# Gates of the mLSTM through the split operands of the projection, the second group's h ahead of a weight split, and two V blocks through other PSUM banks

## The chip, the cores and the metric

One core of a Trainium2 chip runs the whole kernel. The metric is the device time of one execution in microseconds (us). Three executions of the kernel before gave 1976.03, 1974.39 and 1975.19 us; their median is 1975.19 us.

## The reference

One decoder layer (width 2048) for a prompt of 512 tokens and 8 samples of 8 tokens each, 576 tokens in all, in float32:

- `mod = silu(c) @ w_ada + b_ada`, cut into shift, scale and gate. There are 9 different conditions c, one for the prompt and one for each sample.
- `h = rmsnorm(x, norm_pre) * (1 + scale) + shift`, then `u = h @ w_in`. The columns of `u` are q, k, v, z of a differential attention, q, k, v, o, z of an mLSTM, two groups of 4 gate columns `i_m` and `f_m` (input and forget gate of the mLSTM's 4 heads), and two merge gates.
- The attention: 8 heads, two softmax maps each, ALiBi bias; causal within the prompt, and for the samples also over 256 cached keys taken from a paged cache.
- The mLSTM: `ig = i_m + b_igate`, `lf = log_sigmoid(f_m + b_fgate)`, then the recurrence over the tokens with a maximum stabiliser, starting from given states for the samples.
- Both branches are normed, gated and projected, merged by the sigmoids of the merge gates, projected by `w_out`, normed, gated and added to x.

Outputs are the new x, the new K and V rows and the final mLSTM states.

## The kernel before

**Split operands.** A float32 product is computed as three float32r matmuls: each operand is split into a high part (rounded to float32r) and a low part (the difference), and high by high, high by low and low by high are added in PSUM. `h_hi` and `h_lo` hold h as 16 tiles (`kt`) of 128 features by 576 tokens. Weights come in pieces of 256 rows by 256 columns into a ring of 4 slots: SyncE loads `w_raw`, ScalarE writes `w_hi` (`split_hi`), VectorE writes `w_lo` (`split_lo`, line 1514).

**Granules.** One piece is one granule on TensorE (lines 548 to 568): 2 column blocks (`cb`) by 2 row tiles (`t`) by 3 products by 2 halves of 288 tokens, 24 matmuls of 128x128 by 288. All matmuls are issued at line 546.

**The first phase (Q), groups of 4 granules.** h is not known at the start: `mod` is built chunk by chunk from `w_ada`, and chunk j gives shift and scale of the two feature tiles `2j` and `2j+1`. So the Q columns of `w_in` are walked in 8 groups (j = 0 to 7) of 4 granules (`q_granule(n)`, n = 4j + v), group j using tiles `2j` and `2j+1`. ScalarE (group 0) and VectorE (groups 1 to 7, `q_sum`) add each granule's result into `q_acc`. Beside them TensorE runs `ada_round`s, matmuls with 32 columns on one 128x32 strip of the array each (`bank_a`), which read `ada_in` as SyncE has loaded it. Rounds 4 to 7 lie behind granules 0 and 1; rounds 8 to 11 lie behind granule 4, and so on. A finished chunk is copied to `mod_rows` by VectorE (`ss_rows`), transposed by TensorE inside a granule (`ada_rows`, line 595) and folded into `mod_ss` by VectorE (`ss_out`, lines 1570 and 1573). Then `make_h(j)` (VectorE for j = 0 and 1, line 1608 on; GpSimd for j from 2) writes h of two tiles into `h_tmp`, ScalarE writes `h_hi` (`h_hi_pair`) and VectorE writes `h_lo` (`h_low`, line 1579).

**Gates.** `gates(j, ...)` (line 617) multiplies `h_tmp` in plain float32 by the 8 gate columns of `w_in`, padded to 32 (`w_pad`). Its 4 matmuls of 320 tokens go to the four strips of 32 partitions of `bank_s[:, 1]`: two feature tiles by two overlapping halves of the tokens. It stands ahead of the first granule of group j and waits for `h_made`; `make_h(j + 1)` waits for it, since it overwrites `h_tmp`. At granule 28 (`n == QN - 4`) VectorE copies the four strips to `g_rows`, and `gates_tokens` (line 627) adds and transposes them with a 0/1 matrix `g_pick`.

**Order of VectorE at group 0.** For each granule n: `early_lo(n + 3)` first, then in granule 2 `ss_out(1)` and `make_h(1)`, and in granule 3 `h_low(1)` ahead of `early_lo(6)`. ScalarE in granule 3: `h_hi_pair(1)`, then the two copies into `q_acc`, then `split_hi(6)`.

**V blocks and scores.** From x = 88 on (x counts granules of the later phase, 8 a pass p) attention steps are laid between granules: after each granule, transposes of step s-2 into `bank_a` (`weights_t`), the product with V of step s-3 into `bank_o` (`values`), and the scores of step s into both halves of `bank_s` (`scores`); A0 = 93 is step 0. After granules 96 and 97 (p = 12, g = 0 and 1) `to_tokens` also transposes a block of V from `stage` into `bank_s`; VectorE copies it out (`tok_v`, lines 1665 and 1666), and TensorE waits for that copy before the scores of the same step. ScalarE copies `bank_a` to `a_t` (`at_sb`) and `bank_o[:, 0:128]` to `att` (`pv_sb`).

Of the kernel before, what the change touches and what calls it, by code (L numbers as in the profile page):

```python
# [13 lines left out]
P = 128  # L14
# [101 lines left out]
def build(nc, x_prompt, x_sample, cache_k, cache_v, state_C, state_n, state_m, page_table, c_prompt, c_sample,  # L116
# [11 lines left out]
    with ctx:  # L128
# [106 lines left out]
        g_pick = sm("g_pick", [P, 2, 8])  # L235
# [26 lines left out]
        w_pad = sb("w_pad", "ROWS", 2 * KT * 9, [P, KT, 32])  # L262
# [7 lines left out]
        g_rows = sb("g_rows", "WORK", work[0], [P, GSPLIT + NS])  # L270
# [102 lines left out]
        pad_ready = sem("pad_ready")  # L373
        row_out = sem("row_out")
# [169 lines left out]
        def _(pe):  # L544
# [25 lines left out]
            def to_tokens(src, ready, free, dst=None):  # L570

                pe.wait_ge(*ready)
                pe.wait_ge(*free)
                for j in range(NT):
                    nc.tensor.transpose(bank_s[:, 0, j * P:(j + 1) * P], src[:, j * P:(j + 1) * P], ident[:])  # L575
                nc.tensor.transpose(bank_s[0:NS, 1, 0:P], src[:, TP:T], ident[:]).then_inc(dst, 1)
# [40 lines left out]
            def gates(j, jk, start, stop):  # L617

                pe.wait_ge(h_made, 2 * j + 2)
                for t in range(2):  # L620
                    for a in range(2):
                        q = 32 * (2 * t + a)
                        done = mm(bank_s[q:q + 32, 1, 0:GSPLIT + NS], w_pad[:, jk + t, :],
                                  h_tmp[:, t, a * GSPLIT:(a + 1) * GSPLIT + NS], start=start, stop=stop)
                done.then_inc(gates_mm, 1)

            def gates_tokens():

                pe.wait_ge(gate_vec, 1)
                for tt in range(NT + 1):  # L630
                    n, a = (P if tt < NT else NS), tt // 2 if tt < NT else 1
                    done = mm(bank_s[0:n, 0, tt * 8:(tt + 1) * 8], g_rows[:, tt * P - a * GSPLIT:tt * P - a * GSPLIT + n], g_pick[:, a, :])
                done.then_inc(gates_mm, 1)
# [21 lines left out]
            def q_granule(n):  # L655
                j, v = n // 4, n % 4
                if not v:
                    gates(j, 2 * j, j == 0, j == NG - 1)
                pe.wait_ge(h_lo_made, 2 * j + 1)
                pe.wait_ge(lo_ready, n + 1)  # L660
                more, rows_at = j < KG - 1, 1 if j else 2
                granule(n % RING, h_hi, h_lo, 2 * j, True, True, n if n else None, (h_lo_made, 2 * j + 2), j + 1 if v == rows_at and more else None)
                if j == 0 and v < 2:
                    for k in range(AQ + 2 * v, AQ + 2 * v + 2):
                        ada_round(k)
                if v == 0 and j and more:
                    for k in range(n + AQ, n + 2 * AQ):
                        ada_round(k)
# [20 lines left out]
            pe.wait_ge(in_wif, 16)  # L689
# [66 lines left out]
            for x in range(11 * NG, 16 * NG):  # L756
                p, g = x // NG, x % NG
                in_granule(p, g)
                if 0 <= x - A0 - 2 < STEPS:
                    weights_t(x - A0 - 2)  # L760
                if 0 <= x - A0 - 3 < STEPS:
                    values(x - A0 - 3)
                if p in (11, 12) and g < 2:
                    if p == 12:
                        pe.wait_ge(sc_max, x - A0)
                    to_tokens(stage[:, g, :], (bank_free[g], V0 + p), (tok_done, 2 * (p - 5) + g), tok_ps)
                    if p == 12:
                        pe.wait_ge(tok_done, 2 * (p - 5) + g + 1)
                if x == A0:
                    pe.wait_ge(k_kept, HA)  # L770
                if x == 11 * NG + 4:
                    pe.wait_ge(rows_exp, 1)
                    pe.wait_ge(tok_done, 14)
                    for i in range(NT + 1):
                        n = P if i < NT else NS
                        nc.tensor.transpose(bank_s[0:n, 1, 4 * i:4 * i + 4], row_g[:, i * P:i * P + n], ident[0:HM, 0:HM])
                        nc.tensor.transpose(bank_s[0:n, 1, 32 + 4 * i:36 + 4 * i], row_y[:, i * P:i * P + n], ident[0:HM, 0:HM])
                    nc.tensor.transpose(bank_s[0:NB, 1, 64:68], row_s[:, 3 * NS:3 * NS + NB], ident[0:HM, 0:HM]).then_inc(rows_tok_ps, 1)
                    pe.wait_ge(rows_tok, 1)
                if 0 <= x - A0 < STEPS:  # L780
                    scores(x - A0)
# [365 lines left out]
        def _(act):  # L1147
# [30 lines left out]
            act.wait_ge(pad_ready, 1)  # L1178
            act.dma_start(w_pad[:, :, 0:8], w_in2[:, COL_IF:COL_IF + 8].rearrange("(k p) c -> p k c", p=P)).then_inc(in_wif, 16)
# [29 lines left out]
            h_hi_pair(0)  # L1209
            for n in range(QN):  # L1210
# [295 lines left out]
        def _(dve):  # L1506
# [18 lines left out]
            V.memset(w_pad[:], 0.0)  # L1525
# [83 lines left out]
            def make_h(j):  # L1609
# [17 lines left out]
            h_low(0)  # L1627
            for n in range(1, LOOKAHEAD):
                early_lo(n)
            for n in range(QN):  # L1630
                c, v = n // 4, n % 4
                more = c < KG - 1
                if v == 3 and more:
                    h_low(c + 1)
                early_lo(n + LOOKAHEAD)
                if c:
                    q_sum(c, v, n, 0)
                if v == (1 if c else 2) and more:
                    ss_out(c + 1)
                    if not c:  # L1640
                        make_h(1)
# [21 lines left out]
            def tok_v(prompt, sample, n, blk):  # L1663
                dve.wait_ge(tok_ps, n + 1)
                V.tensor_copy(prompt[:, :, bass.ds(blk * P, P)], bank_s[:, 0, :].rearrange("p (a k) -> p a k", a=NT))
                V.tensor_copy(sample[:, bass.ds(blk * P, P)], bank_s[0:NS, 1, 0:P]).then_inc(tok_done, 1)
# [111 lines left out]
            for x in range(11 * NG, 16 * NG):  # L1778
                p, g = x // NG, x % NG
                if p in (11, 12) and g in (1, 2):  # L1780
                    tok_v(v_att, v_smp[0:NS, :], 2 * (p - 5) + g - 1, 2 * (p - 9) + g - 1)
                if x == 11 * NG + 5:
# [366 lines left out]
        def _(pool):  # L2149
# [15 lines left out]
            for a in range(2):  # L2165
                for t in range(2):
                    link(G.affine_select(out=g_pick[:, a, :], in_=g_pick[:, a, :], compare_op=ALU.not_equal, fill=1.0,
                                         base=-32 * (2 * t + a), pattern=[[-1, 8]], channel_multiplier=1))
# [40 lines left out]
            for j in range(2, NG):  # L2209
# [4 lines left out]
                pool.wait_ge(gates_mm, j)  # L2214
# [215 lines left out]
```

## Time and profile before

| | |
|---|---|
| median of 3 executions | 1975.19 us |
| profiled execution, own time | 1976.41 us |
| its span (first to last instruction) | 1974.9 us |
| TensorE busy | 1936.5 us (98%) |
| VectorE, ScalarE, GpSimd busy | 785.2, 642.2, 178.4 us (40%, 33%, 9%) |
| mean granted TensorE clock | 0.997 |

The span begins at the first instruction. "PE" is TensorE's matmuls, "PEld" its weight loads, which run beside the matmuls; the end of a matmul is modelled, so the distance between two starts is what one costs. A plain float32 matmul has two records. In a timeline a row is a run of like instructions, and the bracket gives how long the engine was idle before them and what ended that.

### The profile page before, as it was taken

How to read it: one execution, taken by the hardware profiler on the slowest of the kernel's cores; microseconds unless marked ns; L12 is line 12 of the kernel's file. 1: busy time of each engine (PE TensorE's matmuls, PEld its weight loads, DVE VectorE, ACT ScalarE, POOL GpSimd, SP SyncE). 2: the span in 40 equal slices, each digit the busy share in tenths (PEclk: the TensorE clock that was granted, in tenths of full speed). 3: DMA queues.
4: the chain of work that ended last, by engine and by line, in shares of the span. 5: the costliest groups of instructions: out<-in, count | busy, mean ns of one | idle time of the engine just before them, and what ended most of it. 6: DMA issues, size and time to landing. Idle time of an engine off the chain costs nothing.

```text
span 1974.9 us, 31160 instructions
## 1 busy us (share of the span) xinstructions
PE 1936.5 (98%) x12229; PEld 1661.8 (84%) x12229; DVE 785.2 (40%) x1679; ACT 642.2 (33%) x1144; POOL 178.4 (9%) x308
## 2 busy tenths in 40 slices
PE   6999999999999999999999999999999999999997
PEld 4789898988899998889899988878878878878885
DVE  4665234246553335454445322332332232353224
ACT  4222212235545454343243222222222222333332
POOL 2120012000020101122230000000000000010001
PEclk9999999999999999999999999999999999999998
DMA  9995662231234542223342332232232233353223
GB/s 310 314 290 185 206 225 79 79 107 54 54 121 142 173 138 73 78 82 110 96 131 80 82 84 80 82 103 85 80 104 80 84 102 85 121 189 98 80 81 122
DMA packets 166595, 240.52 MB, mean 122 GB/s; under 512 B 15145, under 2 KB 113577, under 8 KB 165305
## 3 DMA queue, kind: packets, MB, share of 16 engines
q1 hardware_dynamic: 150960, 194.03, 32.7%
q0 software_dynamic: 13264, 44.50, 6.9%
q8 instruction: 91, 1.49, 0.3%
q10 hardware_dynamic: 2242, 0.19, 0.1%
q14 instruction: 38, 0.31, 0.1%
HBM read 220.93 MB, written 17.73 MB: 121 GB/s over the span
## 4 chain that ended last, share of the span: by engine, by line
PE 75%; DVE 1%; POOL 1%; issue 1%; ACT 0%; DVEq 0%; ACTq 0%
PE gemm L546 59%; PE bank_s L546 9%; PE bank_o L546 2%; PE bank_a L546 2%; PE bank_s L795 1%; DVE g_m L2045 1%; DVE y_tok L2126 1%; PE bank_a L741 0%; PE bank_s L960 0%; POOL hm_sq L2343 0%; PE bank_s L1072 0%; POOL hm_sq L2342 0%; ACT hm_sq L1149 0%; PE bank_s L575 0%; DVE y_tok L2073 0%
## 5 line engine op out<-in xcount | busy, mean ns | idle before, releaser
L1514 DVE TENSOR_TENSOR w_lo<-w_raw,w_hi 128x512 fp32r<-128x512 f32 x512 | 358.4, 701 | 780.7 <-ACT w_hi L1149 780.2
L546 PE MATMUL gemm<-h_hi,w_hi 128*128 128x288 f32 (+1 forms) x2560 | 662.3, 324 | 3.5 <-DVE g_m L2045 1.7
L1149 ACT ACTIVATE w_hi<-w_raw 128x512 fp32r<-128x512 f32 x512 | 322.7, 631 | 1021.3 <-PE bank_s L546 568.7
L546 PE MATMUL gemm<-h_hi,w_lo 128*128 128x288 f32 (+1 forms) x2560 | 638.9, 315 | 0.0
L546 PE MATMUL gemm<-h_lo,w_hi 128*128 128x288 f32 (+1 forms) x2560 | 638.0, 314 | 0.0
L546 PEld LDWEIGHTS gemm<-h_hi,w_hi 128*128 128x128 f32 x2560 | 425.1, 189 | 81.4 <-issue 43.1
L546 PEld LDWEIGHTS gemm<-h_lo,w_hi 128*128 128x128 f32 x2560 | 425.5, 188 | 21.1
L546 PEld LDWEIGHTS gemm<-h_hi,w_lo 128*128 128x128 f32 x2560 | 425.8, 188 | 20.3
L546 PE MATMUL gemm<-w_hi,y_all 128*128 128x512 f32 x512 | 158.8, 391 | 0.6 <-DVE g_m L2045 0.6
L546 PEld LDWEIGHTS gemm<-w_hi,y_all 128*128 128x128 f32 x512 | 95.6, 188 | 24.9 <-DVE g_m L2045 1.4
L546 PE MATMUL gemm<-w_lo,y_all 128*128 128x512 f32 x256 | 99.9, 390 | 0.0
L546 PE MATMUL gemm<-brm,w_hi 128*128 128x512 f32 x256 | 79.4, 391 | 0.0
L546 PE MATMUL gemm<-bra,w_hi 128*128 128x512 f32 x256 | 79.4, 391 | 0.0
L2323 POOL DMA_DIRECT2D y_scratch<-g_a x12 | 6.5, 546 | 575.2 <-DVE g_a L2064 574.4
L546 PEld LDWEIGHTS gemm<-bra,w_hi 128*128 128x128 f32 x256 | 47.8, 188 | 11.8
L546 PEld LDWEIGHTS gemm<-brm,w_hi 128*128 128x128 f32 x256 | 47.7, 188 | 11.8 <-issue 0.2
L546 PEld LDWEIGHTS gemm<-w_lo,y_all 128*128 128x128 f32 x256 | 48.1, 188 | 10.2
L1801 DVE CUSTOM_DVE_ANT_0 e_map<-bank_s,alibi 128x128 f32<-128x128 f32 (+3 forms) x64 | 31.5, 492 | 55.3 <-PE bank_s L546 53.8
L546 PE MATMUL bank_s<-w_lo,h_smp 128*64 128x512 f32 x128 | 50.8, 397 | 0.0
L1149 ACT ACTIVATE e_map<-e_map,nmx 128x128 f32<-128x128 f32 (+3 forms) x64 | 35.6, 558 | 46.2 <-DVE nmx L1803 46.2
L546 PE MATMUL gemm<-brm,w_lo 128*128 128x512 f32 x128 | 50.0, 390 | 0.0
L546 PE MATMUL gemm<-bra,w_lo 128*128 128x512 f32 x128 | 50.0, 390 | 0.0
(458 smaller groups left out, 1749.7 us busy)
## 6 DMA issues: line engine op xcount, KB each, us to landing
w_raw<-in_w_in SPq DMA_DIRECT2D x384, 256.0 KB, 2.8
ada_in<-in_w_ada SPq DMA_DIRECT2D x72, 512.0 KB, 7.3
w_raw<-in_w_out SPq DMA_DIRECT2D x64, 256.0 KB, 2.4
ada_gate<-in_w_ada SPq DMA_DIRECT2D x16, 512.0 KB, 5.6
k_page<-in_cache_k POOLq DMA_DIRECT2D x16, 512.0 KB, 5.6
v_page<-in_cache_v POOLq DMA_DIRECT2D x16, 512.0 KB, 4.6
w_raw<-in_w_br_a SPq DMA_DIRECT2D x32, 256.0 KB, 2.4
w_raw<-in_w_br_m SPq DMA_DIRECT2D x32, 256.0 KB, 2.4
```

The lines of the kernel that those rows point to most:

```text
L546: return nc.tensor.matmul(out, lhsT, rhs, start=start, stop=stop, skip_group_check=True)
L795: done = nc.tensor.transpose(bank_s[:, j // 2, (j % 2 * PAGES + pg) * P:(j % 2 * PAGES + pg + 1) * P], k_page[:, pg, h * P:(h + 1) * P], i ...
L1149: return nc.scalar.activation(out, in_, func, **kw)
L1514: V.tensor_tensor(w_lo[:, slot], w_raw[:, slot], w_hi[:, slot], ALU.subtract).then_inc(lo_ready, 1)
L1801: link(V.tensor_tensor_reduce(e_map[:, s % 2, c, 0:n], bank_s[:, c, 0:n], alibi[:, TP - n:TP], 1.0, LOW, ALU.add, ALU.max, mx[:, s % 2, c: ...
L2045: ins = V.scalar_tensor_tensor(g, g, 1.0, gemm[:, b // 2, b % 2, :], ALU.add, ALU.mult)
L2126: V.scalar_tensor_tensor(y_tok[0:n, tt, half], y_tok[0:n, tt, half], rinv[0:n, tt:tt + 1], xa[0:n, half], ALU.mult, ALU.add).then_inc(fin_ ...
L2323: pool.dma_start(y_scratch[4 * i + b], g_a[:, b, :]).then_inc(y_stored, 16)
```

## The change

1. **Gates by split weights.** `w_pad` goes. The 8 gate columns are loaded into `w_if`; ScalarE writes their high part into columns 0 to 7 of `w_if_parts` and VectorE the low part into columns 8 to 15, each once. `gates(j)` now reads `h_hi` and `h_lo`: for two tiles and two halves, one float32r matmul with 16 columns on `h_hi` and one with 8 columns on `h_lo`, 8 in all, of 288 tokens, all to partitions 0 to 15 of the two halves of `bank_s`. It is issued behind the first granule of the group, ahead of the ada rounds. `make_h` no longer waits for it. The copy to `g_rows` is one of 16 partitions by 576, and `g_pick` has 16 rows.
2. **Second group's h.** In granule 2, VectorE does `ss_out(1)` and `make_h(1)` ahead of `early_lo(5)`.
3. **Two V blocks.** At p = 12 the transposes go to `bank_a` (prompt) and `bank_o[:, 128:256]` (samples). They wait for `at_sb` and `pv_sb`; the scores wait for nothing new, and the following `weights_t` waits for VectorE's copy.

```diff
+        w_if = sb("w_if", "ROWS", 2 * KT * 9, [P, KT, 8])
+        w_if_parts = sb("w_if_parts", "ROWS", 2 * KT * 9 + KT * 8, [P, KT, 16], F32R)
@@ TensorE
-            def to_tokens(src, ready, free, dst=None):
+            def to_tokens(src, ready, free, dst=None, banks=(bank_s[:, 0, :], bank_s[:, 1, :]), second=None):
                 pe.wait_ge(*ready)
                 pe.wait_ge(*free)
                 for j in range(NT):
+                    nc.tensor.transpose(banks[0][:, j * P:(j + 1) * P], src[:, j * P:(j + 1) * P], ident[:])
+                if second is not None:
+                    pe.wait_ge(*second)
+                nc.tensor.transpose(banks[1][0:NS, 0:P], src[:, TP:T], ident[:]).then_inc(dst, 1)
-            def gates(j, jk, start, stop):
-                pe.wait_ge(h_made, 2 * j + 2)
-                        done = mm(bank_s[q:q + 32, 1, 0:GSPLIT + NS], w_pad[:, jk + t, :],
-                                  h_tmp[:, t, a * GSPLIT:(a + 1) * GSPLIT + NS], start=start, stop=stop)
+            def gates(j):
+                pe.wait_ge(h_lo_made, 2 * j + 2)
                 for t in range(2):
+                    kt = 2 * j + t
                     for a in range(2):
+                        cols = slice(a * HALF, (a + 1) * HALF)
+                        mm(bank_s[0:16, a, 0:HALF], w_if_parts[:, kt, :], h_hi[:, kt, cols], start=kt == 0, stop=False)
+                        done = mm(bank_s[0:8, a, 0:HALF], w_if_parts[:, kt, 0:8], h_lo[:, kt, cols], start=False, stop=kt == KT - 1)
                 done.then_inc(gates_mm, 1)
@@ q_granule
-                if not v:
-                    gates(j, 2 * j, j == 0, j == NG - 1)
                 ...
                 granule(n % RING, h_hi, h_lo, 2 * j, True, True, n if n else None, (h_lo_made, 2 * j + 2), ...)
+                if not v:
+                    if not j:
+                        pe.wait_ge(w_if_ready, 2)
+                    gates(j)
@@ passes 11 to 15
+                    if p == 12 and 1 <= g < 3:
+                        pe.wait_ge(tok_done, 2 * (p - 5) + g)
                     weights_t(x - A0 - 2)
                 ...
+                if p == 12 and g < 2:
+                    pe.wait_ge(at_sb, x - A0 - 1)
+                    to_tokens(stage[:, g, :], (bank_free[g], V0 + p), (tok_done, 2 * (p - 5) + g), tok_ps,
+                              (bank_a[:], bank_o[:, P:2 * P]), (pv_sb, x - A0 - 2))
@@ ScalarE, after h_hi_pair(0)
+            act.wait_ge(in_wif, 16)
+            go(w_if_parts[:, :, 0:8], w_if[:]).then_inc(w_if_ready, 1)
@@ VectorE, after h_low(0)
+            dve.wait_ge(w_if_ready, 1)
+            V.tensor_tensor(w_if_parts[:, :, 8:16], w_if[:], w_if_parts[:, :, 0:8], ALU.subtract).then_inc(w_if_ready, 1)
@@ VectorE, Q phase
+                if n == 2:
+                    ss_out(1)
+                    make_h(1)
                 early_lo(n + LOOKAHEAD)
-                if v == (1 if c else 2) and more:
+                if c and v == 1 and more:
                     ss_out(c + 1)
-                    if not c:
-                        make_h(1)
-                    V.tensor_copy(g_rows[0:2 * 32, :], bank_s[0:2 * 32, 1, 0:GSPLIT + NS])
-                    V.tensor_copy(g_rows[2 * 32:P, :], bank_s[2 * 32:P, 1, 0:GSPLIT + NS]).then_inc(gate_vec, 1)
+                    V.tensor_copy(halves(g_rows[:]), bank_s[0:16, :, 0:HALF]).then_inc(gate_vec, 1)
@@ make_h on VectorE (if j) and on GpSimd
-                    dve.wait_ge(gates_mm, j)
-                pool.wait_ge(gates_mm, j)
```

## Rows read from the trace of the kernel before

**Rows 1.** Waits of TensorE, whole run: total us, times, longest us.
```profile
PE bank_s L546 <- DVE h_tmp L1624: 3.1, 2, 1.9
PE bank_s L546 <- DVE v_smp L1666: 1.9, 2, 1.0
```

**Rows 2.** Timeline of TensorE around the gates of group 2: start us, length us.
```profile
78.30 0.42 PE L546 MATMUL gemm<-h_hi,w_lo 128*128 128x288 f32 x2
78.65 0.74 PE L546 MATMUL bank_s<-h_tmp,w_pad 128*32 128x320 f32 x8
79.32 0.53 PE L546 MATMUL gemm<-h_hi,w_hi 128*128 128x288 f32 x2
79.69 0.42 PE L546 MATMUL gemm<-h_lo,w_hi 128*128 128x288 f32 x2
```

**Rows 3.** Timeline of TensorE, a later float32r matmul with 64 columns, and the next.
```profile
1403.90 0.40 PE L546 MATMUL bank_s<-w_lo,bra 128*64 128x512 f32 x1
1404.13 0.62 PE L546 MATMUL gemm<-bra,w_hi 128*128 128x512 f32 x2
```

**Rows 4.** Timeline, start of group 0.
```profile
38.03 0.74 PE L546 MATMUL bank_s<-h_tmp,w_pad 128*32 128x320 f32 x8 [1.19 <-DVE h_tmp L1624]
38.70 0.30 PEld L546 LDWEIGHTS gemm<-h_hi,w_hi 128*128 128x128 f32 x2 [0.52 <-DVE h_lo L1579]
```

**Rows 5.** Timeline, the transposes inside granule 2.
```profile
51.38 0.66 PE L595 MATMUL bank_o<-ident,mod_rows 128*128 128x128 f32 x4 [0.36 <-DVE mod_rows L1543]
```

**Rows 6.** Timeline, from granule 2 to granule 5.
```profile
54.86 0.69 DVE L1514 TENSOR_TENSOR w_lo<-w_raw,w_hi 128x512 fp32r<-128x512 f32 x1 [3.53 <-ACT w_hi L1149]
55.47 0.50 DVE L1570 TENSOR_REDUCE mod_ss<-bank_o 128x18 f32<-128x72 f32 x2
56.38 0.43 PE L546 MATMUL gemm<-h_hi,w_lo 128*128 128x288 f32 x2
58.40 0.22 DVE L1624 TENSOR_TENSOR h_tmp<-h_tmp,mod_ss 128x64 f32<-128x64 f32 x1
58.55 1.59 DVE L1579 TENSOR_TENSOR h_lo<-h_tmp,h_hi 128x576 fp32r<-128x576 f32 x2
59.25 1.17 ACT L1149 ACTIVATE q_acc<-gemm 128x576 f32<-128x576 f32 x2
60.02 0.82 PE L546 MATMUL gemm<-h_hi,w_hi 128*128 128x288 f32 x2 [0.60 <-ACT q_acc L1149]
64.88 3.64 PE L546 MATMUL bank_a<-ada_in,c_pad 128*32 128x512 f32 x32
68.45 0.53 PE L546 MATMUL gemm<-h_hi,w_hi 128*128 128x288 f32 x2
```

**Rows 7.** Windows inside granule 4: busy us by engine, granted clock, DMA share, GB/s.
```profile
61.00:62.00 1.00, 1.00 (x6) 1.00 (x5) 1.00 (x2) 0.46 (x1) 0.00 (x0) 0.50 1.08 342
```

**Rows 8.** Loads by tile, the two of round 11: ns, starts; then issue to landing.
```profile
L438 SPq DMA_DIRECT2D ada_in<-in_w_ada x2: 1276/1282/1288, 54.8 to 56.1; - x2
DMA to landing us min/median/max: 9.0/9.3/9.6
```

**Rows 9.** Timeline, end of the Q phase.
```profile
174.40 0.42 PE L546 MATMUL gemm<-h_lo,w_hi 128*128 128x288 f32 x2
174.66 0.43 PE L546 MATMUL gemm<-h_hi,w_lo 128*128 128x288 f32 x2
175.25 0.51 PE L546 MATMUL gemm<-h_hi,w_hi 128*128 128x288 f32 x2 [0.15 <-DVE q_att L1589]
```

**Rows 10.** Timeline behind granule 96.
```profile
422.76 0.47 PEld L575 LDWEIGHTS bank_s<-ident,stage 128*128 128x128 f32 x4
423.20 0.11 PEld L576 LDWEIGHTS bank_s<-ident,stage 128*64 128x64 f32 x1
423.23 0.37 ACT L1149 ACTIVATE a_t<-bank_a 128x256 f32<-128x256 f32 x1
424.55 0.30 PEld L546 LDWEIGHTS bank_s<-k_att,q_att 64*128 64x128 f32 x4 [1.24 <-DVE v_smp L1666]
```

More of the change, by code:

```diff
@@ L234, in build @@
         m_out = sm("m_out", [HM, 1 + NB])
-        g_pick = sm("g_pick", [P, 2, 8])
+        g_pick = sm("g_pick", [16, 8])
         s1 = sm("s1", [P, 2, 9])
@@ L269, in build @@
         tri_bd = wk("tri_bd", [NS, NS])
-        g_rows = sb("g_rows", "WORK", work[0], [P, GSPLIT + NS])
+        g_rows = sb("g_rows", "WORK", work[0], [16, T])
         row_b = wk("row_b", [HM, T])
@@ L373, in build @@
         pad_ready = sem("pad_ready")
+        w_if_ready = sem("w_if_ready")
         row_out = sem("row_out")
@@ L630, in gates_tokens @@
                 for tt in range(NT + 1):
-                    n, a = (P if tt < NT else NS), tt // 2 if tt < NT else 1
-                    done = mm(bank_s[0:n, 0, tt * 8:(tt + 1) * 8], g_rows[:, tt * P - a * GSPLIT:tt * P - a * GSPLIT + n], g_pick[:, a, :])
+                    n = P if tt < NT else NS
+                    done = mm(bank_s[0:n, 0, tt * 8:(tt + 1) * 8], g_rows[:, tt * P:tt * P + n], g_pick[:])
                 done.then_inc(gates_mm, 1)
@@ L762, in _ @@
                     values(x - A0 - 3)
-                if p in (11, 12) and g < 2:
-                    if p == 12:
-                        pe.wait_ge(sc_max, x - A0)
+                if p == 11 and g < 2:
                     to_tokens(stage[:, g, :], (bank_free[g], V0 + p), (tok_done, 2 * (p - 5) + g), tok_ps)
-                    if p == 12:
-                        pe.wait_ge(tok_done, 2 * (p - 5) + g + 1)
+                if p == 12 and g < 2:
+                    pe.wait_ge(at_sb, x - A0 - 1)
+                    to_tokens(stage[:, g, :], (bank_free[g], V0 + p), (tok_done, 2 * (p - 5) + g), tok_ps,
+                              (bank_a[:], bank_o[:, P:2 * P]), (pv_sb, x - A0 - 2))
                 if x == A0:
@@ L1661, in tok_k, with tok_v @@
                 V.tensor_copy(k_tok[0:NS, NT, :], bank_s[0:NS, 1, 0:P]).then_inc(tok_done, 1)
[L1663 removed]
+            def tok_v(prompt, sample, n, blk, banks=(bank_s[:, 0, :], bank_s[:, 1, :])):
                 dve.wait_ge(tok_ps, n + 1)
[L1665 to L1666 removed]
+                V.tensor_copy(prompt[:, :, bass.ds(blk * P, P)], banks[0].rearrange("p (a k) -> p a k", a=NT))
+                V.tensor_copy(sample[:, bass.ds(blk * P, P)], banks[1][0:NS, 0:P]).then_inc(tok_done, 1)
             for g in range(NG):
@@ L1779, in _ @@
                 p, g = x // NG, x % NG
-                if p in (11, 12) and g in (1, 2):
+                if p == 11 and g in (1, 2):
                     tok_v(v_att, v_smp[0:NS, :], 2 * (p - 5) + g - 1, 2 * (p - 9) + g - 1)
+                if p == 12 and g in (1, 2):
+                    tok_v(v_att, v_smp[0:NS, :], 2 * (p - 5) + g - 1, 2 * (p - 9) + g - 1, (bank_a[:], bank_o[:, P:2 * P]))
                 if x == 11 * NG + 5:
@@ L2164, in _ @@
             link(G.memset(g_pick[:], 0.0))
[L2165 to L2168, printed above, removed]
+            for part in range(2):
+                link(G.affine_select(out=g_pick[:], in_=g_pick[:], compare_op=ALU.not_equal, fill=1.0, base=-8 * part,
+                                     pattern=[[-1, 8]], channel_multiplier=1))
             G.memset(eps[:], EPS).then_inc(const_ready, 1)
```

9 lines of the change are left out of this document (1 added, 8 removed).

## The prediction

> **What bounds the kernel now.** The page's busy shares come first: TensorE is busy for 1936.5 of 1974.9 us (98%), so a change pays only by what it takes from TensorE's queue or from its waits. The waits of TensorE are the second view: two of them belong to this change, 3.1 us in two waits for `h_tmp` and 1.9 us in two waits for the V block [rows 1]. They are two thousandths of the span, so the third view is the timeline of each place, where the distance between two starts is read as the cost. All terms below are for the profiled execution, which took 1976.41 us: its span of 1974.9 and 1.5 around it. It lies 1.2 above the median of the three timed runs, 1975.19; what that means is said where the clock comes in.
>
> **Gates, once the phase runs evenly (groups 2 to 7).** From the last pair before them to the second pair behind them 1.39 us pass [rows 2]. Two pairs of 288 tokens account for 0.26 each [rows 9]: 1.39 - 0.53 = 0.86 us a group, of which 0.09 is spent going over to the strips (78.56 to 78.65) and 0.11 coming back (0.37 for the first pair in place of 0.26). The new gates are 8 float32r matmuls of 288 tokens one behind the other on the same partitions. The trace of before has none with 16 or 8 columns. The nearest is one with 64 columns: the next matmul starts 0.23 us later [rows 3], as 512 tokens take at full width. So I take the pitch of the granule's matmuls, 0.13: 8 x 0.13 = 1.05 us. Bounds: 0.12 each if nothing but the streaming counts (0.96), and 0.13 + 0.11 if a weight load as short as that of 64 columns [rows 10] is not hidden (1.9). In groups 2 to 6 the ada rounds follow, which pay their own way onto the strips as before. So +0.19 a group, six groups: **+1.1 us**.
>
> The Trainium skill, "TensorEngine Tiling (Array Packing)", section Theoretical Speedup, speaks against this edit: a left operand of up to 32 columns gains up to four times by packing, and the change gives the packing up. The trace agrees on the packing: 8 records, of which each alone is 0.43 long, stand in 0.74 us [rows 2]. By the rule alone the new gates would cost up to four times as much, 0.74 x 4 = 3.0 us a group, an estimate from that page; but they are also single passes where the old ones were double ones, and [rows 3] gives the price directly.
>
> **Group 0.** The gates stood in a gap: TensorE's first granule waited for `h_lo`, not for them [rows 4], and still starts at 38.70. Behind granule 0 they now cost 1.05. Of that 0.36 is taken up by the wait for `mod_rows` at 51.38 [rows 5], which hangs on weights landing and VectorE's order and not on TensorE. TensorE is then 0.7 late.
>
> **Group 1.** Before: granule 3 ends at 56.38 + 0.26 = 56.64; VectorE had been held by `early_lo(5)`, which itself waited 3.53 us for ScalarE, so `mod_ss` began at 55.47, h was made at 58.62, and granule 4 started at 60.02, at the 0.50 clock [rows 6, 7]. Its 4.86 us to the rounds at 64.88 compare with 24 x 0.13 + 0.1 = 3.3 at full clock: the lower clock cost 1.5 us. After: the transposes end at 52.04 + 0.7 = 52.74 and `mod_ss` starts at 52.8. The same chain of 3.15 us (55.47 to 58.62) ends at 55.95; `early_lo(5)`, now behind it, adds 0.69, and the first half of `h_low(1)` 0.80: 57.44. ScalarE, which makes `h_hi` and only then copies granule 3 out (1.17 for both copies), frees the first bank at about 57.6. TensorE is ready at 57.34, so granule 4 starts at 57.6 with an idle 0.3 in place of 3.4, and the clock stays up. Granule (3.2), gates (1.05) and 0.1 for the strips: the rounds start at 61.95, 2.9 earlier.
>
> What is late next is a DMA. Four rounds take 68.45 - 64.88 = 3.6, 0.9 each [rows 6]. Round 11 would start at 61.95 + 3 x 0.9 = 64.65, but its second half is issued at 56.1 and lands 9.6 us later, at 65.7 [rows 8]; the engines of the DMA are full there (share 1.08, [rows 7]) and this load waits for nothing that the change moves. Before, round 11 started at 67.6 and did not feel it. So the rounds end at 65.7 + 0.9 and granule 5 starts at 66.7 in place of 68.45: **-1.75 us** for groups 0 and 1 together. Bounds: -2.75 if the landing doesn't hold, 0 if h comes no earlier. In an execution where the clock doesn't fall at 60, granule 5 would start at 66.95 already before, and the gain is only 0.25.
>
> **Order of the queues.** `early_lo(5)` is 1.1 later (56.6), and its granule is at 66.7. SyncE's next load into its slot waits for it, but stands behind round 11's loads, of which the last is issued at 56.1 [rows 8], and one more. The loads of rounds 12 to 15 follow round 8, so they move with TensorE. ScalarE's and VectorE's single extra pass over 128 elements a partition fall behind the first h (38.7 to 39.7), and the weights that they then split are not used before granule 1. The gate weights are in SBUF long before. GpSimd's dropped wait for `gates_mm` released nothing: it starts h on `mod_ss`. I cost all of these at nothing; if one of the splits came late, it would show as a wait at a granule, 0.3 at most.
>
> **End of the Q phase.** Granule 30 starts 0.59 after the last pair of 29 where 0.26 would do; VectorE is late with `q_att` because the copies to `g_rows` stand ahead of it [rows 9]. With the last gates behind granule 28, TensorE reaches granule 30 1.05 later against VectorE, and one copy takes the place of two: **-0.3 us** (bounds 0 and -0.4).
>
> **V blocks.** Behind granule 96, 1.79 us pass from the first transpose's load to the scores' (422.76 to 424.55), five loads of 0.11 and then the wait for VectorE [rows 10]. Now the wait stands ahead: `a_t` is copied by 423.60, so the transposes start at 423.65, and the scores' load at 423.65 + 0.55 = 424.20. Queued behind this wait are the transposes and the scores; VectorE, which waits for both, has nothing else due. The wait for `pv_sb` ahead of the fifth is over by then. The gain is 0.35, and granule 97 repeats it: **-0.7 us** (bounds -1.9, if `a_t` were early, and 0).
>
> **Sum.** +1.1 - 1.75 - 0.3 - 0.7 = -1.65: 1976.41 - 1.65 = **1974.8 us** for this execution. If the runs behind the median had the lower clock too, theirs would be 1973.5; if not, 1975.19 - 0.15 = 1975.0. The profiled run is the slowest of the four, which speaks for the second. I stay at 1974.8, which is no change: a measurement of this kernel can tell about 0.2%, 4 us.
>
> **Rivals.**
> - *Slower: the short weight loads are not hidden.* 64 narrow matmuls at 0.11 more each [rows 10]: +7.0, 1981.8. It decides against the change by more than 0.2% from 0.07 each. Against it: the 64-column matmul costs nothing extra [rows 3]. By the Trainium skill, "TensorE: Matmul & The Clock Gate", section LDWEIGHTS, a load's time goes with its columns, so 16 columns would take an estimated 13 ns; no row of before shows it. 6%.
> - *The narrow matmuls put the array into another mode*, as the strips do: 0.09 in and 0.11 out, 8 times, +1.6: 1976.4. The row with 64 columns shows no such gap. 8%.
> - *The clock falls in group 0.* TensorE has nothing from 36.84 (38.03 less its wait of 1.19, [rows 4]) to 38.70, without the old gates in between; at 60 it had fallen after 3.4 us with only the gates in them. Price as at granule 4, +1.5: 1976.3. For it: the gap grows from 1.2 and 0.5 to 1.9 in one. Against: it is a little over half of the other. 10%.
> - *The change doesn't bring h forward*, because ScalarE or VectorE is held elsewhere in granule 2: group 1 keeps its time, +1.75: 1976.5. 8%.
> - *The round's data land earlier*, and the full 2.9 at granule 4 arrives: -1.0, 1973.8. 8%.
>
> **How the numbers follow.** 60% for the forecast. The forecast's own range is 1973.2 to 1976.0, from the median's two readings and the spread of 1.6 us of the timed runs. Taking in the cases at 1976.3 to 1976.5 with that spread, and leaving out the unhidden loads, gives 1972.8 to 1977.6. No case ends below 1971.2, where faster by 0.2% begins: 3% for what I haven't seen. Above 1979.1: 7%, the first rival and a little. Within: 90%.
>
> **What would show it.** The 8 gate matmuls at a pitch of 0.13 and 1.05 us from granule to rounds; no `h_tmp` wait of TensorE; granule 4 at about 57.6 at full clock; a wait for `ada_in` of about 1 us before 66; no gap ahead of granule 30; scores behind granules 96 and 97 at 1.45 in place of 1.79. It is wrong if the gate pitch is 0.2 or more, if the clock is at 0.50 anywhere before 1950 us, or if granule 5 starts after 68.

## The result: 1978.65 us, slower than forecast and slower than before

| | before | after |
|---|---|---|
| median | 1975.97 us (1974.39 to 1976.83) | 1978.65 us (1978.21 to 1980.79) |
| ratio after / before | | 1.0015, 95% interval 1.0009 to 1.0021 |
| span of the profiled execution | 1974.9 us | 1977.1 us |
| TensorE busy | 1936.5 us | 1939.6 us |

The medians are over 22 executions of each kernel. The change costs 2.7 us. The forecast was 1974.8, with a range up to 1977.6. The loss is small but real: the interval excludes 1. The two profiled executions differ by 2.2 us, so their traces show nearly all of it.

The waits of TensorE over the whole run after the change; the columns are those of [rows 1]:

```profile
PE gemm L548 <- DVE q_acc L1597: 2.1, 6, 0.3
PE gemm L548 <- DVE h_lo L1587: 1.9, 1, 1.9
PE bank_a L577 <- ACT a_t L1157: 1.3, 2, 0.6
PE bank_a L548 <- DMA ada_in<-in_w_ada: 0.7, 2, 0.3
```

Both waits of [rows 1], 5.0 us, are gone. The first line is new and was not forecast: six waits of 0.35 us, one for each of groups 2 to 7. The other three are those of the forecast, in new places: the first granule for `h_lo`, the two V blocks for `a_t`, the ada rounds for their weights.

Where the time went is read best as a ledger. The two kernels issue the same matmuls in the same order except for the gates, so each matmul has a start in both traces, and the difference of the two starts can be followed through the run. It changes by 0.1 us or more only at these places (us, minus is earlier; "so far" is the sum up to that line):

```
first matmuls of the run                                          -0.5
granule 0 at the lower clock, then the new gates behind it        +2.6
transposes in granule 2 (their wait is used up)                   -0.5
granule 4 starts at 58.17, not at 60.02                           -1.85 so far
its 1.5 us at the lower clock are gone, its new gates come        -2.3 so far
wait for the weights of an ada round: granule 5 starts            -1.8 so far   (forecast -1.75)
groups 2 to 7: -0.27 where the old gates stood, +1.03 behind
  the first granule = +0.76, six times                            +4.6          (forecast +1.1)
end of the Q phase                                                -0.6          (forecast -0.3)
gates_tokens                                                      +0.2
V blocks: -0.21, -0.19, then +0.25                                -0.15         (forecast -0.7)
end                                                               +2.25
```

One line carries the error. Around granule 8, where [rows 2] stood, the timeline of TensorE after the change is:

```profile
76.52 0.42 PE L548 MATMUL gemm<-h_hi,w_lo 128*128 128x288 f32 x2
77.29 0.50 PE L548 MATMUL gemm<-h_hi,w_hi 128*128 128x288 f32 x2 [0.35 <-DVE q_acc L1597]
77.63 0.42 PE L548 MATMUL gemm<-h_lo,w_hi 128*128 128x288 f32 x2
...
80.28 0.43 PE L548 MATMUL gemm<-h_hi,w_lo 128*128 128x288 f32 x2
80.55 0.29 PE L548 MATMUL bank_s<-h_hi,w_if_parts 128*16 128x288 f32 x1
80.68 0.29 PE L548 MATMUL bank_s<-h_lo,w_if_parts 128*8 128x288 f32 x1
...
81.69 1.06 PE L548 MATMUL bank_a<-ada_in,c_pad 128*32 128x512 f32 x8
```

The new gates cost what they should: a pitch of 0.13, and from 80.55 to 81.69 for eight of them, 0.09 of it for going over to the strips of the rounds, as the rounds did before. But taking the old ones away did not bring 0.86. From the last pair of granule 7 to the second pair of granule 8 there are 77.63 - 76.52 = 1.11 us where two pairs would take 0.53. So 0.58 of the space of the old gates is filled by a wait for VectorE. VectorE's own rows say why:

```profile
74.46 1.42 DVE L1587 TENSOR_TENSOR h_lo<-h_tmp,h_hi 128x576 fp32r<-128x576 f32 x2
75.79 0.69 DVE L1523 TENSOR_TENSOR w_lo<-w_raw,w_hi 128x512 fp32r<-128x512 f32 x1
76.39 1.42 DVE L1597 SCALAR_TENSOR_TENSOR q_acc<-gemm,q_acc 128x576 f32<-128x576 f32 x2
```

Granule 8 begins in the bank of granule 7's first column block. VectorE frees it with the first of the two `q_acc` operations (76.39 and about 0.75 long, so 77.14), behind `h_lo` of the next group and a weight split. The trace of before had the same three operations, and the wait could have been read there:

```profile
76.23 1.42 DVE L1579 TENSOR_TENSOR h_lo<-h_tmp,h_hi 128x576 fp32r<-128x576 f32 x2
77.56 0.69 DVE L1514 TENSOR_TENSOR w_lo<-w_raw,w_hi 128x512 fp32r<-128x512 f32 x1
78.17 1.42 DVE L1589 SCALAR_TENSOR_TENSOR q_acc<-gemm,q_acc 128x576 f32<-128x576 f32 x2
```

Before, the bank came free at 78.17 + 0.75 = 78.92 (0.75 for one of the two, as e2 below shows them apart). From the copy's end to the matmul's start 0.15 passes (77.14 to 77.29 above), so granule 8 could have started at 79.07. It started at 79.32, behind the gates [rows 2]: 0.25 to spare, hence no wait and no row. Without the gates TensorE is ready at 78.30 + 0.26 = 78.56, which is 0.51 too early. After the change it is ready at 76.78 and starts at 77.29: 0.51. The rest of the 0.58 is the first pair behind the wait, 0.34 where 0.26 would do. The bracket's 0.35 is less than 0.51 because it counts from the modelled end of the pair before.

Group 1 went much as forecast, from the early h to the wait for round 11 that takes part of the gain back. After the change (compare [rows 6]):

```profile
56.53 0.22 DVE L1631 TENSOR_TENSOR h_tmp<-h_tmp,mod_ss 128x64 f32<-128x64 f32 x1
58.17 0.50 PE L548 MATMUL gemm<-h_hi,w_hi 128*128 128x288 f32 x2
62.57 2.78 PE L548 MATMUL bank_a<-ada_in,c_pad 128*32 128x512 f32 x24
65.67 1.07 PE L548 MATMUL bank_a<-ada_in,c_pad 128*32 128x512 f32 x8 [0.32 <-DMA ada_in<-in_w_ada]
66.66 0.54 PE L548 MATMUL gemm<-h_hi,w_hi 128*128 128x288 f32 x2
```

Granule 4 starts with no idle time ahead of it. What set it was TensorE itself, late from granule 0, and not ScalarE's copy-out as forecast; in e4 below, where TensorE is not late, it starts at 56.98.

The clock of TensorE fell in granule 0 instead of granule 4, and was back at 1.00 from 43 on. A window of the kernel after, columns as in [rows 7]:

```profile
39.00:40.00 1.00, 1.00 (x7) 1.00 (x6) 1.00 (x3) 0.00 (x0) 0.00 (x0) 0.51 1.10 354
```

### The profile page after: what moved, and what is told of

The parts are those of the page before. It is cut to its first block, busy times and chain, and to the rows that moved or that the text cites. A ratio compares the mean times of both kernels' runs of the same rounds, so it can differ in the third digit from the quotient of the medians.

```text
span 1977.1 us, 31147 instructions
## 1 busy us (share of the span) xinstructions
PE 1939.6 (98%) x12229; PEld 1665.8 (84%) x12229; DVE 784.7 (40%) x1678; ACT 641.8 (32%) x1145; POOL 176.9 (9%) x306
## 4 chain that ended last, share of the span: by engine, by line
PE 92%; DVE 2%; SPq 2%; DMA 1%; issue 1%; POOL 1%; ACT 1%; DVEq 0%; ACTq 0%
PE gemm L548 74%; PE bank_s L548 9%; PE bank_a L548 3%; PE bank_o L548 2%; SPq L440 2%; PE bank_s L803 1%; DVE g_m L2056 1%; DVE y_tok L2137 0%; PE bank_s L577 0%; DMA ada_in<-in_w_ada 0%; PE bank_a L747 0%; DVE q_acc L1597 0%; DVE h_lo L1587 0%; DMA w_raw<-in_w_in 0%; PE bank_s L968 0%
```

## The experiments

Two theories were set against each other for the failed step. *Lost cover*: the old gates stood in a wait of TensorE for VectorE's copy-out, and taking them away uncovers it. *Price of the narrow gates*: 16 and 8 columns, or their place behind a granule, cost more than the trace can show. A second dispute was over groups 0 and 1: does the clock or the landing of round 11 set the start of granule 5? Every kernel was timed beside the kernel before, whose medians there were 1976.29 (e1 to e4), 1976.03 (e5 to e8) and 1976.24 (e9 to e12). "A group" is the drift of a trace over one of groups 2 to 7.

**e1: the new gates ahead of the first granule.** The changed kernel, gates moved back to the old place for groups 2 to 7.

```diff
+                if not v and j > 1:
+                    gates(j)
                 pe.wait_ge(h_lo_made, 2 * j + 1)
                 ...
-                if not v:
+                if not v and j < 2:
```

> The changed kernel with its new gates ahead of the first granule again from group 2 on, in place of behind it. Theory 'lost cover': in the changed kernel TensorE waits 0.5 us at the head of each of groups 2 to 7 for VectorE to free the accumulator bank, 0.59 with the slower first pair, which the old gates had covered by standing there. Then the new gates cover it too: 6 x 0.59 = 3.5 us less than the changed kernel, 0.8 us below the kernel before, and no wait of TensorE for q_acc from group 2 on. Theory 'serial matmuls': the time is lost because eight unpacked matmuls take the place of four packed ones, and the place does not matter: the same time as the changed kernel, 2.7 us above the kernel before.

Measured: 1975.32 (1974.62 to 1976.36), 3.3 less than the changed kernel. There is no wait for `q_acc` from group 2 on, and a group is 0.61 shorter on average. The same eight matmuls in the place of the old gates:

```profile
77.11 0.29 PE L548 MATMUL bank_s<-h_hi,w_if_parts 128*16 128x288 f32 x1
...
78.03 0.30 PE L548 MATMUL bank_s<-h_lo,w_if_parts 128*8 128x288 f32 x1
78.16 0.42 PE L548 MATMUL gemm<-h_hi,w_hi 128*128 128x288 f32 x2
78.42 0.42 PE L548 MATMUL gemm<-h_lo,w_hi 128*128 128x288 f32 x2
```

Granule 8 starts 0.13 behind the last gate, with no idle time. The price is the same 1.05; only the place decides.

**e2: the copy-out first.** The changed kernel, with VectorE's first `q_sum` of granule v = 3 ahead of the weight split.

```diff
+                if c and v == 3:
+                    q_sum(c, v, n, 0)
                 early_lo(n + LOOKAHEAD)
-                if c:
+                if c and v < 3:
                     q_sum(c, v, n, 0)
```

> The changed kernel, and VectorE in the last granule of each group copies the first bank out ahead of the weight split in place of behind it, so that the bank is free 0.7 us earlier; the gates stay behind the first granule. Lost cover: the wait of 0.35 us at the head of groups 2 to 7 goes, 6 x 0.59 = 3.5 us less than the changed kernel (0.8 below the kernel before). Serial matmuls: no change, 2.7 above the kernel before.

Measured: 1975.26 (1974.90 to 1975.66), 3.4 less, with the gates untouched. A group is 0.57 shorter. VectorE and then TensorE in this kernel (`h_lo` starts at 74.46 as in the changed kernel):

```profile
75.79 0.75 DVE L1597 SCALAR_TENSOR_TENSOR q_acc<-gemm,q_acc 128x576 f32<-128x576 f32 x1
76.46 0.68 DVE L1523 TENSOR_TENSOR w_lo<-w_raw,w_hi 128x512 fp32r<-128x512 f32 x1
```

```profile
76.53 0.43 PE L548 MATMUL gemm<-h_hi,w_lo 128*128 128x288 f32 x2
76.79 0.43 PE L548 MATMUL gemm<-h_hi,w_hi 128*128 128x288 f32 x2
77.06 0.42 PE L548 MATMUL gemm<-h_lo,w_hi 128*128 128x288 f32 x2
```

The bank is free at 76.54 instead of 77.14 and granule 8 follows granule 7 at the plain pitch of 0.26. A group now costs 0.76 - 0.57 = 0.19 more than before, which is the forecast's +0.19. Two different edits take the whole loss away, and both act on the wait alone: lost cover holds. In the traces of e1 and e2 the clock stayed at 1.00 in granule 0, where it had fallen in the changed kernel. This has no part in the 3.3 and 3.4: where round 11 starts, e1 is 0.33 later than the changed kernel and e2 level with it, and the gain comes behind that point.

**e3: the old gates behind the first granule.** The kernel before with one move.

```diff
-                if not v:
-                    gates(j, 2 * j, j == 0, j == NG - 1)
                 ...
                 granule(n % RING, h_hi, h_lo, 2 * j, ...)
+                if not v:
+                    gates(j, 2 * j, j == 0, j == NG - 1)
```

> The kernel before with nothing but its old packed float32 gates moved behind the first granule of each group. Lost cover: 0.59 more in each of groups 2 to 7 (3.5), 0.86 less 0.36 in group 0, and up to 0.86 in group 1, where they filled a gap: 4 to 5 us above the kernel before. Serial matmuls: only groups 0 and 1 lose, 0.5 to 1.4 above the kernel before.

Measured: 1978.53 (1976.51 to 1979.72), 2.2 more than before: the move alone, with no new gates, costs nearly what the whole change does. The `q_acc` wait appears in the same form:

```profile
78.55 0.42 PE L546 MATMUL gemm<-h_hi,w_lo 128*128 128x288 f32 x2
79.31 0.51 PE L546 MATMUL gemm<-h_hi,w_hi 128*128 128x288 f32 x2 [0.35 <-DVE q_acc L1589]
```

Groups 2 to 6 lose 0.29 each at the old place and gain 0.54 at the new: +0.25. So the packed gates cost 0.54 there, not 0.86, and that is why the forecast of 4 to 5 us was too high. Group 7 is the exception, and it says what the price hangs on. Behind its first granule no ada rounds follow:

```profile
172.63 0.43 PE L546 MATMUL gemm<-h_hi,w_lo 128*128 128x288 f32 x2
172.99 0.75 PE L546 MATMUL bank_s<-h_tmp,w_pad 128*32 128x320 f32 x8
173.67 0.53 PE L546 MATMUL gemm<-h_hi,w_hi 128*128 128x288 f32 x2
174.04 0.42 PE L546 MATMUL gemm<-h_lo,w_hi 128*128 128x288 f32 x2
```

From the last pair before to the second pair behind them 1.41 us pass, 0.88 more than two pairs: the old price again.

**e4: the clock held up in granule 0.** The changed kernel with 5 instead of 3 identity matmuls ahead of the first granule.

```diff
-            for kt in range(3):
+            for kt in range(5):
                 mm(gemm[:, 0, 0, :], ident[:], xn_t[:, kt, 0:TP])
```

> The changed kernel with five in place of three float32 identity matmuls (their results are not used) ahead of group 0, which fill 1.8 of the 1.9 us in which TensorE waits for the first h. In the changed kernel's trace the clock falls to 0.50 in granule 0. Theory 'the clock cost 1.5 us': 1.5 less than the changed kernel. Theory 'the landing of round 11 sets granule 5': granule 5 starts 0.9 after the load lands at 65.7 whatever the clock did ahead of it, so the same time as the changed kernel within 0.3, with a longer wait of TensorE for ada_in.

Measured: 1978.78 (1977.34 to 1981.22), no change. The clock stayed at 1.00, the rounds behind granule 4 started at 61.38 instead of 62.57, and the wait took it all back:

```profile
61.38 2.78 PE L548 MATMUL bank_a<-ada_in,c_pad 128*32 128x512 f32 x24
65.83 1.06 PE L548 MATMUL bank_a<-ada_in,c_pad 128*32 128x512 f32 x8 [1.67 <-DMA ada_in<-in_w_ada]
```

Granule 5 starts at 66.83 here and at 66.66 with the lower clock. The landing of round 11's weights sets it, as the forecast said, and the 1.5 us of the lower clock are covered by it.

**e5: e3 with the copy-out first.** The edits of e3 and of e2 on the kernel before.

> The kernel before with its old packed gates behind the first granule, and VectorE copying the first bank out ahead of the split in the last granule of each group. In the run with the old gates behind and the old order a group cost 0.25 us more than before. Lost cover: the uncovered wait and slower first pair, 0.57 a group, go: -0.32 a group and 3.4 less than that run, 1.2 below the kernel before. If the 0.25 had another cause than the wait: 2.2 above the kernel before, as that run.

Measured: 1975.80 (1974.35 to 1977.39), 2.7 under e3 where 3.4 was expected, and 0.55 less a group in the trace. Against the kernel before it is 0.2 lower, where 1.2 was expected and the single executions of both spread over 3 us. The wait explains the old gates' loss as well; the size is confirmed by the trace and not by the medians.

**e6: the second group's h, alone.** The kernel before with part 2 of the change only.

> The kernel before with only the second part of the change: second group's h ahead of the weight split. Landing theory: granule 5 can't start before about 66.6, 0.9 after round 11's load has landed at 65.7, so it gains at most the 1.8 us to 68.45, and 0.3 where the clock did not fall in the kernel before: 0.3 to 1.8 below it. Theory 'h was the bound': granule 4 starts near 57 and all 2.9 to 3.4 us arrive.

Measured: 1975.33 (1973.64 to 1976.43), 0.7 under before, which the runs can't tell from nothing. Granule 4 starts at 57.08 at full clock and the rounds 4.4 earlier than before; the landing takes 1.6 of this back:

```profile
60.45 2.78 PE L546 MATMUL bank_a<-ada_in,c_pad 128*32 128x512 f32 x24
64.70 1.07 PE L546 MATMUL bank_a<-ada_in,c_pad 128*32 128x512 f32 x8 [1.47 <-DMA ada_in<-in_w_ada]
```

Round 11's weights come 1 us earlier here than in the changed kernel, in a trace that is 0.4 ahead of before's already at granule 2. The landing is fixed against the edits here, but its place moves by about 1 us from one trace to the next. The profiled execution is the fastest of the eleven, so its trace shows more (2.8) than the median.

**e7: two loads earlier.** e2, and SyncE issues the two loads of round 8 ahead of the next piece of `w_in`.

```diff
+            for k in (2 * AQ, 2 * AQ + 1):
+                ada_load(k)
             for n in range(QN):
                 w_load(n + LOOKAHEAD + RING)
                 if n % 4 == 0:
-                    for k in range(n + 2 * AQ, min(n + 3 * AQ, ADA_N)):
+                    for k in range(n + 2 * AQ + (0 if n else 2), min(n + 3 * AQ, ADA_N)):
                         ada_load(k)
```

> The run with VectorE's copy-out first, and SyncE issues the loads of rounds 8 and 9 ahead of the weight load of granule 7, which has to wait for a split; the DMA engines were idle for about 2 us there (share 0.27 from 48 to 50). Landing theory: round 11's data land up to 2 us earlier, TensorE's wait of 1.5 us for ada_in goes and granule 5 starts at about 65.2: 1.5 less than that run, 2.5 below the kernel before. If the landing does not set granule 5: no change against that run.

Measured: 1974.63 (1973.13 to 1975.33), 0.6 under e2, beside medians of before that differ by 0.3; its trace is 2.0 shorter. The mechanism is there, the four rounds run unbroken:

```profile
61.13 3.64 PE L550 MATMUL bank_a<-ada_in,c_pad 128*32 128x512 f32 x32
```

and granule 5 starts at 64.70. In the medians it is 0.6 where 1.5 was expected. The single executions say where the rest is. Five took 1973.13 to 1973.84 us, with a mean granted clock of 0.998 (0.997 in one); six took 1974.63 to 1975.33, with 0.996 or 0.997. One fall of the clock to 0.50 for 3.4 us, as in the traces, lowers the mean by 0.001. The profiled execution is of the first five, and its clock did not fall. In e2, five executions at 0.998 and six at 0.997 have the same time (medians 1975.26 and 1975.16). So the early loads bring 1.9 where the clock stays up (1.6 without the difference of the two medians of before), and a fall that the landing had covered now costs 1.4. This is read from a rounded third digit and not from traces of the six: that the clock fell there, and in granule 0, is likely and not shown.

**e8 and e12: what works, together.** The kernel before with its packed gates behind the first granule (e3), h early (e6), the copy-out first (e2) and the loads of e7. No split gates, no edit of the V blocks.

> The kernel before with the old packed gates behind the first granule, the second group's h early, the copy-out first and the two round loads ahead; no split gates and no V edit. Old gates behind the granule cost 0.53 a group (they share the strips with the ada rounds that follow), the new ones 1.03: 8 x 0.5 = 4.0 less than the new gates with the same rest, so 6.5 below the kernel before, 1969.8. If the packed gates are no cheaper there: as the run with the loads ahead, 2.5 below.

> The best kernel so far once more, beside the other kernels of this call: 1971.4 us, 0.23% under the kernel before, whose 1976.0 the same runs give.

Measured: 1971.38 (1970.09 to 1972.05), ratio to before 0.9978 (0.9968 to 0.9987); once more 1971.17 (1969.85 to 1971.43), 0.9973 (0.9963 to 0.9984). It beats both kernels, and misses the forecast of 1969.8 by 1.6. It is 3.3 under e7, from which it differs by the packed gates and by the V blocks (0.2 the other way). In the traces the packed gates are worth 0.50 in each of groups 1 to 6 and 0.2 in group 7, where no rounds follow: 3.2, where the forecast took 8 x 0.5. The gates of group 2 in e12:

```profile
78.73 0.74 PE L548 MATMUL bank_s<-h_tmp,w_pad 128*32 128x320 f32 x8
79.29 3.19 PE L548 MATMUL bank_a<-ada_in,c_pad 128*32 128x512 f32 x28
```

The rounds start 79.29 - 78.73 = 0.56 behind the gates, which are 0.74 long by the record.

**e9: the copy-out first in the kernel before.** The edit of e2 and nothing else.

> The kernel before, with VectorE's copy-out of the last granule of each group (q_sum) ahead of the weight split (early_lo); gates stay where they were, ahead of the first granule. Lost cover (the copy-out is late only for a TensorE that has no gates in front of its next granule): there is no wait for q_acc in the kernel before, so bringing the copy-out forward frees nothing: 1976.0 us, no drift in groups 2 to 7, below 0.1 us a group. Rival (the copy-out by itself slows the first pairs of each group, gates or no gates): 0.3 to 0.5 us less in each of six groups, about 1973.5 us.

Measured: 1975.72 (1974.90 to 1976.90), ratio 0.9998 (0.9989 to 1.0007), where the rival asked for about 1973.5. Over groups 2 to 7 no matmul drifts by more than 0.12 us against the trace of before. The reordering is worth 3.4 us in one kernel and nothing in the other, as a covered wait should be. This is the counter-test that the theory needed.

**e10: e8 with five identity matmuls.** The edit of e4 on the best kernel.

> The best kernel so far (packed gates behind the first granule, h of the second group early, q_sum first, two loads earlier) with five identity matmuls instead of three ahead of the first granule. In that kernel's trace the clock fell to 0.50 in granule 0 and 1.5 us went there; the wait for the weights of the ada rounds that hid this in the changed kernel is gone. If a longer run of matmuls ahead of the first granule keeps the clock up: granule 0 at full clock, up to 1.5 us less in executions in which it fell, 1970 to 1971 us. Rival (the clock falls or not from execution to execution, and two more matmuls cost their own time or nothing): no change, 1971.4 us.

Measured: 1970.42 (1969.61 to 1971.01), 0.75 under e12, ratio to before 0.997 (0.9958 to 0.9982). The window of e12 and then that of e10, 40 to 41 us:

```profile
40.00:41.00 1.00, 1.00 (x6) 1.00 (x5) 0.38 (x1) 0.43 (x1) 0.00 (x0) 0.50 1.11 357
```

```profile
40.00:41.00 1.00, 1.00 (x10) 1.00 (x9) 0.10 (x1) 0.65 (x1) 0.00 (x0) 1.00 1.10 365
```

The rounds behind granule 0 start at 42.10 instead of 43.90. Of these 1.8 us, 0.84 are left at the rounds behind granule 4 (60.95 against 61.79). Two places took the rest back, 0.28 at granule 2 and 0.61 at its transposes, and both show as waits: 0.22 for `q_acc` of ScalarE and 0.48 for `mod_rows`. The rounds of e10 are 0.3 ahead from the start, so about 0.6 of the clock's 1.5 is left. With the landing out of the way the clock costs something, though not all of it. The two medians have overlapping ranges. But the mean granted clock was 0.998 in all six executions of e10 and 0.997 in all eight of e12: this agrees with a clock that the longer run of matmuls keeps up in every execution.

**e11: e8 with the V blocks of the change.**

> The best kernel so far (its V blocks are those of the kernel before) with the change's edit of the two V blocks added. Ledger of the changed kernel (the edit gains 0.2 behind each of granules 96 and 97 and gives 0.2 back at the wait that it adds ahead of the following transposes): -0.2 us from granule 95 to 100, no measurable change of the time, 1971.2. Prediction's price: -0.7, 1970.7.

Measured: 1970.35 (1969.84 to 1971.25), ratio 0.9971 (0.9959 to 0.9982), 0.8 under e12, which the overlapping ranges don't separate; the trace places only 0.2 of it. Three of its seven executions had a mean clock of 0.998 and took 1969.84 to 1970.18; the four at 0.997, which is the clock of all of e12, have a median of 1970.89, 0.3 under e12. So most of the 0.8 seems to go with the clock and not with the V blocks. Behind granule 96, e12 and then e11:

```profile
417.77 0.60 PE L577 MATMUL bank_s<-ident,stage 128*128 128x128 f32 x4
419.45 1.13 PE L548 MATMUL bank_s<-k_att,q_att 64*128 64x512 f32 x4 [0.97 <-DVE v_smp L1671]
```

```profile
418.68 0.66 PE L577 MATMUL bank_a<-ident,stage 128*128 128x128 f32 x4 [0.61 <-ACT a_t L1155]
419.38 1.13 PE L548 MATMUL bank_s<-k_att,q_att 64*128 64x512 f32 x4
```

The wait moves from behind the transposes to ahead of them and shrinks from 0.97 to 0.61. Against e12 the scores come 0.22 earlier behind granule 96 and 0.17 behind 97; then the transposes behind granule 98, where `weights_t` has the added wait, come 0.19 later. The same three steps as in the changed kernel's ledger: -0.2 in all.

## Why the prediction was wrong

- **The step that failed: "Gates, once the phase runs evenly".** It took 0.86 us a group as removed. Only 0.27 came off, because TensorE came 0.51 too early for VectorE's copy-out and restarts slowly behind it. Six times 0.58 is the 3.5 between the forecast's +1.1 and the measured +4.6. With 0.27 in place of 0.86 the forecast's own sum would have given 1978.3, beside 1978.62 for the profiled execution. e1 and e2 each recover 3.3 to 3.4 us, and e9 shows that the same wait does not exist under the old gates. The text asked "what is late next" for group 1 and for the end of the Q phase, and not here, in the only term that counts six times.
- **Right, the price of the new gates.** 1.05 us a group; the ledger shows 1.03. The rivals of unhidden weight loads and of another mode were wrong. The loads take 95 ns (16 columns) and 88 ns (8 columns), and are hidden behind a pitch of 131. The Trainium skill, "TensorE: Matmul & The Clock Gate", section LDWEIGHTS, has the load's time go with its columns, which gave an estimate of 13 ns; the rows of after disagree, and 8 columns fewer save 7 ns:

```profile
L548 PEld LDWEIGHTS bank_s<-h_hi,w_if_parts x32: 94/95/98, 42.9 to 174.1; 128*16 128x16 f32 x32
L548 PEld LDWEIGHTS bank_s<-h_lo,w_if_parts x32: 87/88/88, 43.0 to 174.2; 128*8 128x8 f32 x32
```

- **Right in part, "the change gives the packing up".** Priced at +0.19 a group against the old place, it is also 0.50 a group against the same packed gates in the new place, where ada rounds follow (e12 against e7). The forecast never set the new gates against the old ones behind the granule, where they share the way onto the strips with the ada rounds. The Trainium skill, "TensorEngine Tiling (Array Packing)", section Theoretical Speedup, gives up to four times for packing; here the old form costs about half of the new, 0.54 against 1.03. That is not the page's factor, since the two also differ in format, columns and tokens; no run here has the same matmuls packed and not packed.
- **Right, groups 0 and 1 together.** Granule 5 at 66.66, forecast 66.7; granule 4 at 58.17, forecast 57.6, though for another reason than forecast (see above). e4 and e6 confirm the landing as the limit. It came out right although two parts did not: TensorE was 0.6 later at the rounds than forecast (62.57, not 61.95) because of the clock, and waited 0.3 for the data instead of about 1.
- **The clock rival came true and cost nothing.** It was given +1.5 and 10%. The clock fell in granule 0 of the profiled execution, but the landing of round 11 absorbs it, as the comparison with e4 shows. A clock of 0.50 was also named as a sign of being wrong; it is not what made the forecast wrong. The rival and the landing stood in the same text and were not combined. Their order decides: a delay ahead of a fixed arrival is free as long as it is shorter than the wait for it (1.67 us in e4). e7, e10 and e11 show the price once the wait is gone.
- **End of the Q phase: the right mechanism**, -0.3 forecast. Granule 30 follows with no gap, which gives -0.4; the other 0.2 of the measured -0.6 is a slow drift over granules 28 to 31 that belongs to no wait.
- **V blocks: mis-sized.** Forecast -0.35 each; measured -0.21, -0.19, and +0.25 for the wait that the change adds to the following `weights_t`. That wait stands in the description of the change and had no price in the sum:

```profile
425.59 0.37 ACT L1157 ACTIVATE a_t<-bank_a 128x256 f32<-128x256 f32 x1
426.01 0.66 PE L577 MATMUL bank_a<-ident,stage 128*128 128x128 f32 x4 [0.61 <-ACT a_t L1157]
426.70 0.30 PEld L548 LDWEIGHTS bank_s<-k_att,q_att 64*128 64x128 f32 x4 [0.20 <-issue]
```

  The transposes start about 0.05 behind the copy, as forecast, and the scores' load 0.69 later, not 0.55.
- **The range.** It left 7% above 1979.1 for one rival that turned out false. The measured 1978.65 lies between that and the upper end of 1977.6, where no case stood. The true cause had no share in the chances at all.

Open: why the clock falls in some executions and not in others behind the same wait.

## What to carry to other kernels

A wait that is covered has no row in a profile. Before counting removed work as gained, take every releaser that the engine would meet earlier by that amount, read when it finishes in the trace of before, and subtract: here 0.25 us of slack against a move of 0.76 us, from three rows. Do it first for the term that repeats most. Then look for the fixed arrivals, such as a load that waits for nothing that is changed: a gain ahead of them is worth nothing beyond the point at which they land, and a loss costs nothing while it is shorter than the wait, until they move.

## What was not expected of the hardware

- **Packed matmuls next to other packed ones are cheaper than alone.** The eight records of the old gates cost 0.86 us between full-width matmuls [rows 2] and 0.54 (e3) or 0.56 (e12) ahead of the ada rounds, which use the same kind of strips. Within e3, too, they cost 0.54 where rounds follow and 0.88 in group 7, where none do. Ahead of the rounds, these start before the gates' records end (79.29 against 79.47 in e12). That the ways onto the strips and back are shared is argued from this, not shown.
- **Narrow weight loads hardly get shorter.** Float32r loads take 88 ns for 8 columns and 95 for 16 (rows above), 134 for 64 (`bank_s<-w_lo,bra` in the trace of before) and 188 for 128 on the page of the profile. The 0.11 us of [rows 10] is a load for a transpose, of which one with 128 columns takes about 0.14.
- **The lower clock comes in some executions and not in others, for the same wait.** Behind an idle time of TensorE ahead of granule 0, the granted clock fell to 0.50 between 39 and 40 in the changed kernel (idle 1.9 us), e3 (2.1), e8 (2.1), e11 (2.4) and e12 (2.2), and stayed at 1.00 in e1 (1.9), e2 (1.7), e5 (2.2) and e7 (2.1). It fell at 60 before. Behind an idle time of 3.2 us ahead of granule 4 it fell at 61 in e5 and not in e3, and it did not fall in e9, whose gap there is that of before. Each of these is one execution. Where it fell it was 0.50 for 3.4 us and cost about 1.5 us of TensorE's time.
